# A fused two-block transformer kernel on one Trainium2 core: the swapped halves of the rotary tiles come from transfers within SBUF, begun on GpSimd, and no longer from products with a permutation matrix

## The reference

```python
def rope(t, pos):
    half = t.shape[-1] // 2
    inv = ROPE_THETA ** (-jnp.arange(half, dtype=jnp.float32) / half)
    ang = pos.astype(jnp.float32)[..., None, None] * inv
    cos, sin = jnp.cos(ang), jnp.sin(ang)
    t1, t2 = tf[..., :half], tf[..., half:]          # tf is t in fp32
    return jnp.concatenate([t1 * cos - t2 * sin, t2 * cos + t1 * sin], axis=-1)
...
    c_q, c_kv, k_pe = jnp.split(b_part, [MLA_Q_LORA, MLA_Q_LORA + MLA_KV_LORA], axis=-1)
    qfull = (rmsnorm_2(c_q, mla_q_norm) @ mla_w_uq).reshape(B, S, B_HEADS, MLA_NOPE + MLA_ROPE)
    q_b = jnp.concatenate([qfull[..., :MLA_NOPE], rope(qfull[..., MLA_NOPE:], pos)], axis=-1)
    kv = (rmsnorm_2(c_kv, mla_kv_norm) @ mla_w_ukv).reshape(B, S, B_HEADS, MLA_NOPE + MLA_V)
    k_rot = jnp.broadcast_to(rope(k_pe[:, :, None, :], pos), (B, S, B_HEADS, MLA_ROPE))
```

## Time and profile before

| | |
|---|---|
| time of three runs | 3227.48 us median (3226.89 to 3227.84) |
| span of the profiled execution, first to last instruction | 3226.3 us (the page gives this one time for that execution) |
| PE busy | 3183.2 us, 99% of the span |
| DVE / ACT / POOL busy | 1879.4 us (58%) / 512.8 us (16%) / 231.0 us (7%) |
| mean granted PE clock | 0.996 |
| transfers | 288.31 MB, mean 89 GB/s |

### The profile page before, as it was taken

One profiled execution on the slowest core, in us unless ns is written; L12 is line 12 of the kernel. 1 busy time (PEld: TensorE's weight loads), 2 busy tenths in 40 slices (PEclk: granted clock), 3 DMA queues, 4 the chain that ended last, 5 costly groups with the idle time before them and its releaser, 6 DMA issues.

```text
span 3226.3 us, 36432 instructions
## 1 busy us (share of the span) xinstructions
PE 3183.2 (99%) x14382; PEld 2591.5 (80%) x14382; DVE 1879.4 (58%) x3268; ACT 512.8 (16%) x1080; POOL 231.0 (7%) x206
## 2 busy tenths in 40 slices
PE   9999999999999999999999999999999999999999
PEld 3888758888888888884488888888888854788888
DVE  6356845764347764464776664466644647766643
ACT  2111122000011000105521000110001145210001
POOL 1244400000000000003000000000000030000000
PEclk9999999999999999999999999999999999999999
DMA  5254321222222222223012222222222230122221
GB/s 237 89 173 161 135 70 53 92 80 90 92 82 92 82 85 85 90 72 124 1 64 81 92 86 88 89 83 87 88 85 88 74 124 1 53 92 88 82 84 61
DMA packets 43882, 288.31 MB, mean 89 GB/s; under 512 B 5404, under 2 KB 5404, under 8 KB 12736
## 3 DMA queue, kind: packets, MB, share of 16 engines
q1 hardware_dynamic: 39024, 271.14, 24.2%
q0 software_dynamic: 4688, 14.85, 1.4%
HBM read 281.76 MB, written 2.11 MB: 88 GB/s over the span
## 4 chain that ended last, share of the span: by engine, by line
PE 91%; DVE 5%; DVEq 1%; ACT 1%; issue 1%; DMA 0%; ACTq 0%; POOL 0%
PE ps L831 76%; PE ps L550 3%; PE ps L1274 2%; PE ps L966 1%; PE ps L1242 1%; PE ps L1185 1%; DVE arena L1888 1%; PE ps L531 1%; PE ps L858 1%; PE ps L931 1%; DVE arena L2310 1%; ACT arena L1586 1%; PE ps L1256 1%; DVEq L2323 1%; PE ps L1281 0%
## 5 line engine op out<-in xcount | busy, mean ns | idle before, releaser
L831 PE MATMUL ps<-arena 128*128 128x256 f32 x5456 | 1244.9, 379 | 0.1
L831 PEld LDWEIGHTS ps<-arena 128*128 128x128 f32 x5456 | 1036.6, 190 | 141.5 <-DVE arena L2061 0.5
L831 PE MATMUL ps<-arena,ring 128*128 128x256 f32 x2768 | 646.1, 379 | 0.5 <-ACT arena L1314 0.5
L831 PEld LDWEIGHTS ps<-arena,ring 128*128 128x128 f32 x2768 | 525.7, 190 | 72.4 <-ACT arena L1314 0.9
L831 PE MATMUL ps<-xn,ring 128*128 128x256 f32 x2272 | 518.8, 379 | 5.8 <-DVE arena L1704 2.3
L831 PEld LDWEIGHTS ps<-xn,ring 128*128 128x128 f32 x2272 | 431.2, 190 | 71.9 <-issue 9.4
L1698 DVE TENSOR_TENSOR arena<-arena,ps 128x512 f32<-128x512 f32 x173 | 118.9, 687 | 553.3 <-PE ps L831 494.4
L1671 DVE TENSOR_TENSOR arena<-ring 128x512 f32<-128x512 f32 (+1 forms) x194 | 131.1, 676 | 347.5 <-PE ps L831 347.3
L831 PE MATMUL ps<-xn,arena 128*128 128x256 f32 x1264 | 302.2, 379 | 0.0
L831 PEld LDWEIGHTS ps<-xn,arena 128*128 128x128 f32 x1264 | 240.2, 190 | 32.6
L1502 ACT ACTIVATE arena<-arena 128x512 f32<-128x512 f32 x88 | 55.4, 630 | 883.3 <-DVE arena L2180 883.3
(11 more groups left out here) (321 smaller groups left out, 2510.9 us busy)
## 6 DMA issues: line engine op xcount, KB each, us to landing
ring<-in_w_up_a SPq DMA_DIRECT2D x44, 1024.0 KB, 4.9
ring<-in_w_up_b SPq DMA_DIRECT2D x44, 1024.0 KB, 4.9
ring<-in_w_ff SPq DMA_DIRECT2D x32, 1024.0 KB, 4.9
ring<-in_w_ada SPq DMA_DIRECT2D x24, 1024.0 KB, 5.0
ring<-in_w_down_a SPq DMA_DIRECT2D x16, 1024.0 KB, 4.9
ring<-in_w_down_b SPq DMA_DIRECT2D x16, 1024.0 KB, 4.9
ring<-in_w_in SPq DMA_DIRECT2D x14, 1024.0 KB, 4.9
ring<-in_w_out SPq DMA_DIRECT2D x12, 1024.0 KB, 5.3
```

The source lines that it names most:

```text
L831: mm = nc.tensor.matmul(out_ap, w, operand(product, quads[i]), start=at not in opened, stop=last_chunk and i == len(quads) - 1, skip_group ...
```

## The change

The three products with `swap` in each layer are gone. In their place GpSimd begins 8 transfers of 16 partitions x 512 values (32 KB) for each rotary tile; they write the swapped tile to `square_of[:, t, :]`, the buffer that `rope` used for its temp. `rope` multiplies that buffer in place by the sines, where it read a PSUM bank before, and waits for the 8 transfers (a count of 128) and not for a product. The keys' transfers start once both kv tiles are normalised; the queries' stand behind the three `window` loads and ahead of the three `bias` additions. The banks and counts of the "turn" places stay as they were: `rope` still raises them.

```diff
+            def halves_swapped(dst, src, name):
+                half = ROPE // 2
+                for at in range(0, P, 2 * half):
+                    for a, b in ((at, at + half), (at + half, at)):
+                        nc.gpsimd.dma_start(dst[a:a + half, :], src[b:b + half, :]).then_inc(sem(name), 16)
...
+                pool.wait_ge(sem("kv_normed"), KV_TILES * layer + KV_TILES)
+                halves_swapped(square_of[:, 0, :], proj[:, PE_IN, :], "keys_swapped")
                 pool.wait_ge(sem("roped"), layer + 1)
...
                 for n in range(3):
                     window(layer, n)
+                for t in range(2):
+                    wait_evacuated(pool, "uq", t, layer=layer)
+                    halves_swapped(square_of[:, t, :], qr[:, t, :], f"queries_swapped{t}")
                 pool.wait_ge(sem("zeros"), 4 * layer + 4)
                 for n in range(3):
                     bias(layer, n)
...
-                def turn_keys(bank0):
-                    pe.wait_ge(sem("projected"), 14 * layer + PE_IN + 1)
-                    nc.tensor.matmul(ps[:, bank0 + 3, :], swap, proj[:, PE_IN, :], start=True, stop=True)\
-                        .then_inc(sem("swapped"), 1)
-                    return {3: (sem("roped"), layer + 1)}
-                def turn_queries(u):
-                    if u in (3, 5):
-                        t = u // 2 - 1
-                        wait_evacuated(pe, "uq", t, layer=layer)
-                        wait_bank(pe, "turn", t, layer=layer)
-                        nc.tensor.matmul(bank_ap("turn", t), swap, qr[:, t, :], start=True, stop=True)\
-                            .then_inc(sem("swapped"), 1)
...
-                pe_product(pe, "uq", lambda k: proj[:, Q_IN + k, :], layer, turn_queries)
+                pe_product(pe, "uq", lambda k: proj[:, Q_IN + k, :], layer)
...
-                def rope(dst, count, bank, temp):
-                    dve.wait_ge(sem("swapped"), count)
-                    nc.vector.tensor_tensor(temp, ps[:, bank, :], sin_t, ALU.mult)
+                def rope(dst, name, temp):
+                    dve.wait_ge(sem(name), 16 * (P // (ROPE // 2)) * (layer + 1))
+                    nc.vector.tensor_tensor(temp, temp, sin_t, ALU.mult)
...
                 for t in range(2):
-                    b = BANKS + bank("turn", t, 0, 0, layer)[0]
-                    rope(qr[:, t, :], 3 * layer + 2 + t, b, square_of[:, t, :]).then_inc(evacuated("turn", t), 1)
+                    if t == 1:
+                        wait_evacuated(dve, "uq", 3, layer=layer)
+                    rope(qr[:, t, :], f"queries_swapped{t}", square_of[:, t, :]).then_inc(evacuated("turn", t), 1)
```

More of the change, by code:

```diff
@@ L1146, in _ @@
                         seven("in", layer, p, UP_QUADS, up_operand, operand_ready(3 * layer + 1), "aefdcbg", by_quads=True)
-                    elif p in (1, 3, 4, 5):
+                    elif p in (1, 3, 4):
                         ahead = {1: row_sums(("m", layer, DT, ssq[:, :])), 3: row_sums(("q", layer, 3, ssq[:, :])),
-                                 4: row_sums(("kv", layer, 2, ssq[:, :])), 5: turn_keys}[p]
+                                 4: row_sums(("kv", layer, 2, ssq[:, :]))}[p]
                         seven("in", layer, p, UP_QUADS, up_operand, None, "ebdgcaf", ahead=ahead)
@@ L2245, in _ @@
                     elif p == 5:
-                        rope(proj[:, PE_IN, :], 3 * layer + 1, 4 * half_of(number) + 3, square_of[:, 0, :])\
+                        rope(proj[:, PE_IN, :], "keys_swapped", square_of[:, 0, :])\
                             .then_inc(sem("roped"), 1)
```

## The result

| | time, median of 5 runs | span of the profiled execution | mean granted PE clock |
|---|---|---|---|
| before | 3227.84 us (3226.89 to 3229.68) | 3226.3 us | 0.996 |
| after | 3238.89 us (3238.68 to 3240.33) | 3237.0 us | 0.995 |

The changed kernel takes 1.0035 times as long (95% interval 1.0025 to 1.0046), 11.05 us more; the spans differ by 10.7 us. 3237.3 us was forecast.

A forecast was written before the change was run, and what follows sets the result against it. PE, with 91% of the ending chain, was taken to bound the kernel. +3.2 us a layer (+6.4) and +3.4 for the clock made +9.8 on the 3227.5 us median: 3237.3 us, 8-in-10 range 3227.5 to 3242.

The forecast's parts named there:

- What bounds it: PE holds 91% of the ending chain; "uk" tile 0, which may not start before query tile 0's rotation, is to be watched.
- Keys, -0.86 a layer: Key product leaves the chain, 0.86 us a layer; its eight transfers land with at least 3.6 us of cover.
- POOL's issues: Sixteen query transfers at 0.50 us each keep POOL until 1469.6; only then can the three additions start.
- Landing: Query tile 0's last transfer, behind POOL's loads and beside a weight load, lands at about 1470.8, bracket 1468.6 to 1471.2.
- the 0.4 us for the landing: Term added after tile 0's last query transfer has moved: 2.0 us less 1.0 to first packet less the transfer itself.
- The additions hold DVE: Query tile 0's rotation steps wait on POOL's additions until 1478.0; PE idles 5.8 us before "uk", net +3.2 us a layer.
- All three steps meet an addition each: Query tile 0's three rotation steps take turns with POOL's three additions, one step after each, ending at 1478.0.
- each of the three steps should take over 1 us: Sign expected in DVE's rotation of query tile 0, with POOL's additions between 1469 and 1478.
- Clock: After PE's idling the clock falls in "uk" and "uv": 0 to 3.4 us a layer, 1.7 taken, +3.4 us for both.
- A: Query swaps beat the load and additions at tile 0's rotation: 3229.1 us, up to 3234 with a clock fall; chance 0.23.
- B: Nothing waits: query rotation ends by 1472.4, all three products a layer are won, 5.2 us, 3222.3 us; chance 0.04.
- C: 16-partition transfers so slow that query tile 1 is late too, or the keys hold DVE: 3247 us; chance 0.05.

The follow-up runs named there:

- banks free: Changed kernel, with the removed products' two bank places given free by the copies of "uq" tiles 0 and 3, not by the rotation: 3222.94 us.
- swaps first: Changed kernel, with the sixteen query transfers begun ahead of the three loads: 3223.04 us; together with banks free 3222.27 us.
- Idle ahead: Changed kernel, with GpSimd also waiting for ScalarE's copy of "uq" tile 4 ahead of the first of the three additions: 3237.06 us.
- gap filled: Changed kernel, with six products that nobody reads put between "uq" and "uk": 3234.35 us.

## Why the prediction was right

- **What bounds it.** "uk" waiting for the rotation through its bank was named as the place to watch; PE's idle rows have it there, 5.71 and 5.70 us (forecast 5.8), and banks free, which wins 5.0 of the 5.2 us without that wait, leaves no other place of any size.
- **Keys, -0.86 a layer.** Right; two products less is 1.6 us measured. The last transfer was begun at 1407.6 and landed 1.8 us later, so some 5 us of cover were left up to the rotation at 1414.61, more than the 3.6 that I counted on.
- **POOL's issues.** 0.484 us each and not 0.50, so the additions began at 1468.77; this run is 0.49 us ahead of the kernel before, in whose times I worked (its "uq" starts at 1456.46, there at 1456.95), so 1469.3 in those times against a forecast of 1469.6.
- **Landing.** The first step began at 1470.54, or 1471.0 in the times of the kernel before; 1470.8 forecast. The cause given, the loads in front and the weight load, fits swaps first, which does not part the two. One term doesn't follow from its rows: the 0.4 us for the landing would be 2.0 - 1.0 - 0.19 = 0.8, or 1468.0 - 1467.4 = 0.6. Choosing 1470.8 out of a wide bracket hid it.
- **The additions hold DVE: right in size, wrong in manner.** "All three steps meet an addition each" failed: one step met all three. Its sign "each of the three steps should take over 1 us" did not come: they took 5.74, 0.68 and 0.69 us. The end hardly moves, because three additions have to pass in either order: 1477.64 measured, 1478.1 in the times of the kernel before, 1478.0 forecast, and a net +3.1 us a layer beside +3.2. The sentence that any start gives that end "within 0.6 us" carried the number through the wrong picture, so the number's agreement says nothing for the picture. Idle ahead then showed steps of 2.7 to 2.8 us in turn with the additions, as I had drawn them, in a kernel where GpSimd pauses.
- **Clock.** Taken at 1.7 us a layer, the middle between 0 and 3.4, because neither end was nearer to a row; it was 1.54 and 2.69. That it came so close is luck as much as reasoning. These 0.8 us in all are nearly the whole difference between the forecast span, 3236.1, and 3237.0; gap filled gives the whole price of the clock back by keeping PE busy.
- **Rivals.** A (the swaps beat the additions) appears only in kernels that reorder GpSimd; B (all six products won, 3222.3 us) asked for a rotation that ends by 1472.4; the two kernels with swaps first have it for tile 0 (at about 1467) and come to 3223.0 and 3222.3 us. Banks free alone comes to 3222.9 us in a way that the prediction did not list, with the step held and nobody waiting for it. C did not happen.

## What to carry to other kernels

When an operation is moved off the bounding engine, look at what its old result released: here a PSUM bank that nothing wrote any more still made PE wait for the slow replacement, and releasing it early turned a loss of 11 us into a gain of 5. An operation that reads two SBUF tiles on VectorE should not be due while GpSimd works through a row of instructions on SBUF: moving three additions behind it took 14 us off here, though they must not come so late that the next work waits for them. And a stall of the bounding engine is to be priced with its aftermath: 5.7 us of idling cost 1.5 to 2.7 us more at half clock here.

## What the runs showed of the hardware

- A VectorE step with two SBUF inputs stayed shut out through the rest of three GpSimd additions in a row (it took 4.9 to 6.1 us in five kernels whose additions followed the transfers at once), also with a 0.1 us memset between them; with GpSimd idle for 2.1 us ahead it was let in after each.
- A GpSimd drain behind sixteen transfers stood for 7.1 to 7.6 us, whether VectorE worked or not; between additions, with those transfers landed, 0.16 us.
- TensorE's granted clock stayed up after idle gaps of 0.6 to 2.35 us ahead of "uk" and fell to half, the 1.2 GHz level, after 5.7 and 7.3 us; the same products took 7.0 to 7.1 us or 8.6 to 9.8. In all of these PE had run "uq" without a gap before it idled. In the attention, whose products leave gaps, half speed followed an idle gap of 1.81 us.
- Transfers of 16 partitions landed in 1.7 to 1.8 us each with the queue quiet (the keys' eight), and in 5.8 to 7.2 us behind 1.5 MB of loads and beside a weight load of 1 MB (the queries' sixteen).
